# Hybrid decoder step: the sample's page items in the merged attention plan, in one run per round

## The chip, the cores and the metric

One core of a Trainium2 chip runs one launch of the kernel. Its engines are PE (TensorE: matmul and transpose), DVE (VectorE), ACT (ScalarE), POOL (GpSimd) and SP (SyncE, which here issues DMAs). Each engine works through its own list of instructions in order and waits on semaphores for the others. The metric is the time of one execution in microseconds (us); the time before is 1838.18 us, the median of three runs (1833.62 to 1845.4).

## What is computed

One layer of a hybrid decoder over a prompt of 1024 tokens and a sample group of 8 sequences with 8 new tokens each, which read 2048 cached tokens in 16 pages of 128. All inputs are fp32.

```
h_n = rmsnorm(h);  z = h_n @ w_in                    # q,k,v,gates,indexer and HGRN columns
# A: indexer scores pick the top 256 causal keys, then softmax attention over them
s = einsum('bthd,btkhd->bthk', q, k_sel) * HEAD_DIM ** -0.5
p = softmax(where(valid, s, -inf));  att = einsum('bthk,btkhd->bthd', p, v_sel)
# prompt: keys are its own 1024 tokens; sample: 2048 paged cache tokens and its 8 new ones
# B: HGRN2 gated recurrence over chunks, per head a 128 x 128 state
y = sigmoid(ma) * ((att * silu(ga)) @ w_a) + sigmoid(mb) * ((rmsnorm(o) * silu(hg)) @ w_b)
h = h + rmsnorm(y @ w_o);  h = h + sigmoid(h @ w_pg) * (p_i @ w_pp)
```

The kernel does not gather keys: it adds a bias of 0 or -1e30 to the scores and computes attention over all keys up to the diagonal.

## The kernel before

The program runs in stages: norm and transposes of the input, the indexer with its top-k on DVE while PE computes the gate projections, the projections of q, k and v, then **attention**, then HGRN2, merge, and output. The change touches attention only.

**The plan.** Attention is written out as one list `plan` of entries (kind, number, part). PE, ACT and DVE each walk through this one list and do their own part of each entry, so the list sets the order on all three engines.

The prompt's part goes over 32 pairs `att_pairs` (a tile i of 128 queries, and a pair of heads k). They come in groups of eight, tiles 7 and 0 in turn, then 6 and 1, 5 and 2, 4 and 3, so a wide and a narrow pair alternate; tile i has i + 1 blocks of 128 keys. A pair m has two heads, 2m and 2m + 1, called steps. For it:

- Q(m): PE computes the scores of both heads (L1017) and adds the bias (L1022) in four PSUM banks. It waits for both exponentials of pair m - 1, which read the same banks.
- E(2m), E(2m+1): DVE takes the row maximum (L1661, L1662), ACT the exponential with its sum (L1426) into one of three SBUF buffers.
- N(2m), N(2m+1): DVE takes the reciprocal (L1666) and scales the row (L1668).
- T(n, 0), T(n, 1): PE transposes up to four blocks of step n (L1042); ACT copies part 0 out of PSUM (L1432), DVE part 1 (L551), which only tiles 4 to 7 have.
- A(m): when the transposed blocks of both steps are copied, PE multiplies with the values (L1051), and ACT copies the result.

The sample's part is a list `smp_plan` for eight sequences b: K(b, page), PE transposes a page of keys (L1059), copied by ACT (even pages, L1432) or DVE (odd pages, L539); S(b, c), scores against four pages (L1071, L1073), copied by DVE (L542), which also takes a maximum (L1682); X(b), the exponential of the whole row on ACT (L1430, 2112 columns), after a small DVE maximum (L1670, L1671); P(b, c), PE transposes four blocks (L1082), copied by ACT; V(b, c), PE multiplies with four pages of values (L1095); M(b), DVE scales and masks the result (L1676), which PE waits for in O(b) (L1100).

**The ring.** K, S, P, O, T and A write to a ring of three PSUM banks in the order of the plan: PE may start an entry only when the entry three before it has been copied out by its keeper.

**Pages.** SP loads the pages of K, eight ahead, as PE finishes with them (L562); POOL loads the pages of V in the same way. Neither list of loads depends on how prompt and sample are mixed.

**Mixing.** `some(share)` appends sample entries to the plan until they have come as far as the sum of shares given; a round gives 8 shares, and there are 256 entries (without M and X, which come along free) for 32 rounds, so a round takes eight. Round m holds Q(m) and E, N of its steps, the T of the steps of pair m - 1, and A(m - 1).

Of the kernel before, what the change touches and what calls it, by code (L numbers as in the profile page):

```python
# [61 lines left out]
def hybrid_layer(nc, x_p, x_s, p_p, p_s, ck, cv, cki, st, pt, g_pre, g_post, w_in, lbl, hg_g, w_a, w_b, w_o,  # L62
                 w_pg, w_pp, y_p, y_s, k_p, v_p, ki_p, s_p, k_s, v_s, ki_s, s_s):
    with ExitStack() as ctx:
# [313 lines left out]
        NA, NM = len(att_steps), len(att_pairs)  # L378
# [61 lines left out]
        def turns(n):  # L440

            return [("T", n, q) for q in range(att_steps[n][0] // 4 + 1)]

        plan = []
# [3 lines left out]
        def some(share):  # L448

            given[0] += share  # L450
            while given[1] < len(smp_plan) and (sum(e[0] not in "MX" for e in smp_plan[:given[1] + 1])
                                                <= given[0] * n_smp / (8 * NM) or smp_plan[given[1]][0] in "MX"):
                plan.append(smp_plan[given[1]])
                given[1] += 1
        for m in range(NM + 1):
            if m < NM:
                plan += [("Q", m, 0), ("E", 2 * m, 0)]
            some(1)
            plan += turns(2 * m - 2) if m else []
            if m < NM:  # L460
                plan += [("E", 2 * m + 1, 0)]
            some(2)
            if m < NM:
                plan += [("N", 2 * m, 0)]
            plan += turns(2 * m - 1) if m else []
            some(2)
            if m < NM:
                plan += [("N", 2 * m + 1, 0)]
            plan += [("A", m - 1, 0)] if m else []
            some(3)  # L470
        assert given[1] == len(smp_plan)


# [1358 lines left out]
```

How the kernel before makes its waits and increments, by code:

```python
            def run(ins, s_):  # L518
                count[s_.name] = count.get(s_.name, 0) + 1
                ins.then_inc(s_, 1)
                eng.wait_ge(s_, count[s_.name])
# [10 lines left out]
        def ring_copy(eng, run, copy, e):  # L532
            kind, a, x = e
            o, done = ring_bank(e), ring_kept(e)[0]
            eng.wait_ge(sem("ring2_full"), ring_no[e] + 1)
            if kind == "K":
                c = x // 4
                run(copy(KTb[c % 2][:, :, P * (x % 4):P * (x % 4) + P], o.rearrange("p (k t) -> p k t", k=HP)), done)
# [24 lines left out]
        def idx_load(eng, b):  # L564
            for g in range(NPG):
                if b >= NPI and g % 4 == 0:
                    eng.wait_ge(sem("ring_full"), RB + smp_no["T", b - NPI, g // 4] + 1)
                r = eng.value_load(pt_sb[0:1, b * NPG + g:b * NPG + g + 1], min_val=0, max_val=cki.shape[1] - 1)
                eng.dma_start(pgi[b % NPI][:, g, :], cki[0][bass.ds(r, 1), :, :].rearrange("a p d -> p (a d)"))\
                   .then_inc(sem(f"idx_pages{b % NPI}"), 16)
# [27 lines left out]
            def units_to(n):  # L600
                nonlocal nu
                for u in range(nu, min(n, len(units))):
                    mat, kc, c, w = units[u]
                    if u >= NW:
                        sp.wait_ge(*raw_free(u - NW))
                    sp.dma_start(wbuf[u % NW][:, 0:kc, 0:w],
                                 mat[0].rearrange("(k p) n -> p k n", p=P)[:, :, c:c + w])\
                      .then_inc(sem(f"unit_load{u % NW}"), 16)
```

## Time and profile before

| what | before |
|---|---|
| median of three runs | 1838.18 us |
| profiled execution, its time / its span | 1830.32 us / 1828.7 us |
| PE busy | 1640.7 us (90%) |
| DVE busy | 1016.0 us (56%) |
| ACT busy | 466.9 us (26%) |
| POOL busy | 401.1 us (22%) |
| mean granted PE clock | 0.959 of full speed |

The profile is one execution. "Busy" counts instructions in work; matmuls are pipelined, so a busy PE is not PE at its peak. PEld, where it appears, is PE loading the stationary operand, which overlaps its matmuls. The granted clock is the share of 2.4 GHz that PE was allowed; it is 1.0 or 0.5 at any moment. In a row of the timeline, the bracket at the end gives the idle time of the engine before the instruction and what ended it.

### The profile page before, as it was taken

What the parts mean: (1) busy time and instruction counts of PE and PEld (TensorE: products, weight loads), DVE (VectorE), ACT (ScalarE), POOL (GpSimd) and SP (SyncE); (2) the same over time, 40 slices, a digit from 0 to 9 for tenths busy, and PEclk for the clock granted to TensorE, in tenths of its full rate; (3) what the DMA queues carried; (4) which work ended last, traced back from release to release, by engine and by line L of the source; (5) the groups of instructions that cost most, each with busy time, mean ns of one, the idle gap of its engine ahead of it and who ended that gap; (6) DMA issues with size and microseconds to landing.
All of it is one profiled execution on the core that took longest, in us unless ns stands there. A gap on an engine that the chain in (4) does not pass through costs nothing.

```text
span 1828.7 us, 27255 instructions
## 1 busy us (share of the span) xinstructions
PE 1640.7 (90%) x10006; PEld 1259.6 (69%) x10026; DVE 1016.0 (56%) x1778; ACT 466.9 (26%) x816; POOL 401.1 (22%) x431
## 2 busy tenths in 40 slices
PE   3978789999999999997888888877997998999997
PEld 2964569999999999996555555557894663444442
DVE  7258469999999998101556666646963321111111
ACT  5147432223111111011344444541025000101010
POOL 5301333543223223241011121112610000000000
PEclk9988889999999999998889999988998999999999
DMA  5100211223322223013555666624035620010010
GB/s 159 39 6 6 51 38 67 89 96 132 108 96 96 95 96 105 24 50 131 176 175 183 220 218 220 222 85 169 1 88 207 240 96 29 26 52 26 26 45 17
DMA packets 105894, 183.04 MB, mean 100 GB/s; under 512 B 21537, under 2 KB 62050, under 8 KB 105762
## 3 DMA queue, kind: packets, MB, share of 16 engines
q1 hardware_dynamic: 93474, 145.64, 23.7%
q0 software_dynamic: 12288, 35.66, 6.2%
q8 instruction: 80, 1.31, 0.3%
q14 instruction: 52, 0.43, 0.1%
HBM read 147.43 MB, written 33.83 MB: 99 GB/s over the span
## 4 chain that ended last, share of the span: by engine, by line
PE 77%; DVE 10%; issue 5%; ACT 5%; DMA 1%; SPq 0%; POOLq 0%; POOL 0%; ACTq 0%; DVEq 0%; another core or an unknown queue 0%
PE PS L891 36%; PE PS L1233 7%; PE PS L1261 7%; PE PS L898 6%; PE PS L1059 3%; PE PS L1114 2%; DVE buf L1574 2%; PE PS L1256 2%; PE PS L1017 2%; PE PS L1051 2%; PE PS L1071 1%; ACT buf L1432 1%; PE PS L1095 1%; DVE buf L1661 1%; PE PS L1042 1%
## 5 line engine op out<-in xcount | busy, mean ns | idle before, releaser
L891 PE MATMUL PS<-hn_hi,w_hi 128*128 128x384 f32 (+3 forms) x1080 | 353.3, 327 | 6.3 <-issue 6.3
L891 PE MATMUL PS<-hn_lo,w_hi 128*128 128x384 f32 (+3 forms) x1080 | 353.4, 327 | 0.0
L891 PE MATMUL PS<-hn_hi,w_lo 128*128 128x384 f32 (+3 forms) x1080 | 353.4, 327 | 0.0
L1604 DVE TENSOR_SCALAR_CACHE_REDUCE buf<-buf,buf 128x384 f32<-128x384 f32 (+3 forms) x224 | 258.9, 1156 | 8.0
L891 PEld LDWEIGHTS PS<-hn_hi,w_hi 128*128 128x128 f32 (+1 forms) x1080 | 202.4, 187 | 7.2 <-issue 6.5
L891 PEld LDWEIGHTS PS<-hn_lo,w_hi 128*128 128x128 f32 (+1 forms) x1080 | 202.5, 187 | 0.7
L891 PEld LDWEIGHTS PS<-hn_hi,w_lo 128*128 128x128 f32 (+1 forms) x1080 | 202.4, 187 | 0.7
L562 POOL DMA_DIRECT2D buf<-in_cache_v_dram x128 | 70.0, 547 | 332.9 <-PE PS L1095 230.2
L1233 PE MATMUL PS<-buf,buf 128*128 128x512 f32 (+1 forms) x288 | 127.0, 600 | 7.0 <-DVE buf L1789 3.8
L1432 ACT ACTIVATE buf<-PS 128x512 f32<-128x512 f32 (+4 forms) x200 | 101.6, 508 | 101.4 <-PE PS L1059 45.5
L779 POOL CAST w_hi<-buf 128x2048 fp32r<-128x2048 f32 (+1 forms) x27 | 54.2, 2009 | 329.3 <-DMA buf<-in_w_in_dram 200.5
L1661 DVE TENSOR_REDUCE buf<-PS 128x1 f32<-128x1024 f32 (+7 forms) x64 | 48.5, 758 | 139.4 <-PE PS L1022 127.8
L1261 PE MATMUL PS<-buf,buf 128*128 128x512 f32 (+1 forms) x288 | 125.1, 592 | 0.0
L780 POOL TENSOR_TENSOR w_lo<-buf,w_hi 128x2048 fp32r<-128x2048 f32 (+1 forms) x27 | 124.4, 4607 | 2.2
L891 PE MATMUL PS<-buf,buf 128*128 128x384 f32 (+1 forms) x384 | 118.8, 473 | 4.8 <-ACT buf L1466 4.8
L1059 PE MATMUL PS<-buf,buf 128*128 128x128 f32 x512 | 83.3, 303 | 29.0 <-ACT buf L1432 19.0
L891 PEld LDWEIGHTS PS<-buf,buf 128*128 128x128 f32 x384 | 73.7, 192 | 50.5 <-ACT buf L1466 5.8
L1233 PEld LDWEIGHTS PS<-buf,buf 128*128 128x128 f32 (+1 forms) x288 | 53.3, 186 | 79.2 <-issue 70.9
L1261 PEld LDWEIGHTS PS<-buf,buf 128*128 128x128 f32 (+1 forms) x288 | 53.0, 184 | 70.6 <-issue 70.6
L1393 ACT ACTIVATE buf<-PS 128x768 f32<-128x768 f32 x28 | 22.8, 814 | 284.9 <-PE PS L891 284.9
L1059 PEld LDWEIGHTS PS<-buf,buf 128*128 128x128 f32 x512 | 61.4, 153 | 47.1 <-issue 36.2
L1803 DVE TENSOR_TENSOR buf<-PS,buf 128x1024 f32<-128x1024 f32 (+1 forms) x9 | 11.0, 1223 | 144.9 <-ACT buf L1497 144.9
(255 smaller groups left out, 2669.5 us busy)
## 6 DMA issues: line engine op xcount, KB each, us to landing
buf<-in_cache_v_dram POOLq DMA_DIRECT2D x128, 256.0 KB, 4.1
buf<-in_cache_k_dram SPq DMA_DIRECT2D x128, 256.0 KB, 4.1
buf<-in_w_in_dram SPq DMA_DIRECT2D x26, 1024.0 KB, 6.1
gates_scratch<-buf SPq DMA_DIRECT2D x40, 544.0 KB, 3.1
buf<-gates_scratch SPq DMA_DIRECT2D x40, 544.0 KB, 6.2
buf<-in_x_prompt_dram SPq DMA_DIRECT2D x16, 512.0 KB, 4.1
out_dram<-buf SPq DMA_DIRECT2D x2, 2048.0 KB, 8.0
buf<-in_w_out_dram SPq DMA_DIRECT2D x1, 4096.0 KB, 16.6
```

What stands on the lines that cost most here:

```text
L562: eng.dma_start(dst, cache[0][bass.ds(r, 1), :, :, :].rearrange("a p h d -> p (a h d)")).then_inc(s_, 16)
L779: run(nc.gpsimd.tensor_copy(hi, raw), s_)
L780: run(nc.gpsimd.tensor_tensor(lo, raw, hi.bitcast(fp32), ALU.subtract), sem("w_split"))
L891: last = mm(ps[0:min(w, P), 512 * j:512 * j + tn], wt[:, k, P * half:min(w, P * half + P)], xt_[:, k, t0:t0 + tn], start=m == 0, stop=m == ...
L898: last = mm(ps[0:r, WC * j:WC * j + w], xt_[:, k, P * i:P * i + r], wt[:, k, 0:w], start=m == 0, stop=m == len(steps) - 1)
L1017: mm(bank(2 * e, 2)[:, c:c + w], qT[p0:p0 + 64, k, P * i:P * i + P], KT[p0:p0 + 64, k, c:c + w], start=True, stop=False)
L1059: last = tr(o[:, k, :], kpage[n % NKP][:, P * k:P * k + P], ident)
L1233: last = mm(bank(c)[0:r, :], mixT[:, k, P * i:P * i + r], wo[:, k, 512 * c:512 * c + 512], start=k == 0, stop=k == KD - 1)
L1261: last = mm(bank(4 + c)[0:r, :], hT[:, k, 0:r], wpg[:, k, 512 * c:512 * c + 512], start=k == 0, stop=k == KD - 1)
L1432: ring_copy(act, run, lambda o, i: A(o, i, ACT.Copy), e)
L1604: run(V.tensor_scalar(junk[0:r, 0:v.shape[1]], v, t, None, op, ALU.add, accum_out=CN[0:r, j:j + 1]), ch)
L1661: run(V.tensor_reduce(mx[:, q:q + 1], bank(2 * (b % 2), 2)[:, 0:nk], AX.X, ALU.max), ch)
```

## The change

In each round the shares 1, 2, 2 and 3, which stood at four places between the prompt's entries, become one run of 8 shares at the end of the round, after A(m - 1). N(2m) follows E(2m + 1) directly. The set of entries is the same, and so is the order within the prompt's and within the sample's entries.

```diff
         for m in range(NM + 1):
             if m < NM:
                 plan += [("Q", m, 0), ("E", 2 * m, 0)]
-            some(1)
             plan += turns(2 * m - 2) if m else []
             if m < NM:
-                plan += [("E", 2 * m + 1, 0)]
-            some(2)
-            if m < NM:
-                plan += [("N", 2 * m, 0)]
+                plan += [("E", 2 * m + 1, 0), ("N", 2 * m, 0)]
             plan += turns(2 * m - 1) if m else []
-            some(2)
             if m < NM:
                 plan += [("N", 2 * m + 1, 0)]
             plan += [("A", m - 1, 0)] if m else []
-            some(3)
+            some(8)
```

The changed file is five lines shorter from there on, so that L1017 of before is L1012 after, and so on. Buffers in the rows below: 49 is the identity, 131 the queries (and attention outputs), 132 the keys, 134 to 136 the three probability buffers, 137 and 138 their transposed copies, 139 and 140 the transposed key pages, 141 and 142 the transposed sample probabilities, 143 the sample's probability row.

PE in round 14 (m = 14, tile 6), from the first matmul behind Q(14) on. Before:

```order
L1095 MATMUL PS<-buf_161,buf_142 32x128 x4
L1095 MATMUL PS<-buf_162,buf_142 32x128 x4
L1095 MATMUL PS<-buf_163,buf_142 32x128 x4
L1095 MATMUL PS<-buf_164,buf_142 32x128 x4
L1042 MATMUL PS<-buf_49,buf_136 128x128 x2
L1082 MATMUL PS<-buf_49,buf_143 64x128
L1071 MATMUL PS<-buf_132,buf_175 32x64 x4
L1073 MATMUL PS<-buf_114,buf_55 128x64
L1042 MATMUL PS<-buf_49,buf_134 128x128 x2
L1095 MATMUL PS<-buf_133,buf_141 32x128 x4
L1059 MATMUL PS<-buf_49,buf_169 128x128 x4
L1051 MATMUL PS<-buf_137,buf_133 64x128
```

After, from the same place on:

```order
L1037 MATMUL PS<-buf_49,buf_136 128x128 x2
L1037 MATMUL PS<-buf_49,buf_134 128x128 x2
L1046 MATMUL PS<-buf_137,buf_133 64x128
L1046 MATMUL PS<-buf_138,buf_133 64x128
L1046 MATMUL PS<-buf_137,buf_133 64x128
L1046 MATMUL PS<-buf_138,buf_133 64x128
L1090 MATMUL PS<-buf_161,buf_142 32x128 x4
L1090 MATMUL PS<-buf_162,buf_142 32x128 x4
L1090 MATMUL PS<-buf_163,buf_142 32x128 x4
L1090 MATMUL PS<-buf_164,buf_142 32x128 x4
L1077 MATMUL PS<-buf_49,buf_143 64x128
L1066 MATMUL PS<-buf_132,buf_175 32x64 x4
```

Before, V, T(26) (buf_136), P, S, T(27) (buf_134), V and K stand between Q and A(13), whose first matmul is the last row (L1051, buf_137); after, the two T stand there alone, A (L1046) follows, and then V, P, the second V (not shown) and four K.

ACT in the same round and into round 15. Before (L1426 is E, L1430 is X):

```order
L1426 ACTIVATE buf_136,buf_147<-PS,buf_146 128x896
L1432 ACTIVATE buf_141<-PS 64x128
L1432 ACTIVATE buf_138<-PS 128x256
L1430 ACTIVATE buf_143,buf_151<-buf_143,buf_150 128x2112
L1432 ACTIVATE buf_139<-PS 128x4x128
L1432 ACTIVATE buf_131<-PS 128x128
L1432 ACTIVATE buf_139<-PS 128x4x128
L1426 ACTIVATE buf_134,buf_147<-PS,buf_146 128x256
L1432 ACTIVATE buf_137<-PS 128x512
L1426 ACTIVATE buf_135,buf_147<-PS,buf_146 128x256
L1432 ACTIVATE buf_141<-PS 128x512
L1432 ACTIVATE buf_138<-PS 128x512
```

After (L1421 is E, L1425 is X):

```order
L1421 ACTIVATE buf_136,buf_147<-PS,buf_146 128x896
L1427 ACTIVATE buf_138<-PS 128x256
L1427 ACTIVATE buf_131<-PS 128x128
L1427 ACTIVATE buf_141<-PS 64x128
L1425 ACTIVATE buf_143,buf_151<-buf_143,buf_150 128x2112
L1427 ACTIVATE buf_139<-PS 128x4x128 x2
L1421 ACTIVATE buf_134,buf_147<-PS,buf_146 128x256
L1427 ACTIVATE buf_137<-PS 128x512
L1421 ACTIVATE buf_135,buf_147<-PS,buf_146 128x256
L1427 ACTIVATE buf_138<-PS 128x512
L1427 ACTIVATE buf_131<-PS 128x128
L1427 ACTIVATE buf_141<-PS 128x512
```

In round 14 the copy of T(27) (to buf_138) came after the sample's P copy (to buf_141) and now comes before it; in round 15 the P copy (to buf_141) that stood between the second exponential and T(29)'s copy to buf_138 now comes after A's copy (to buf_131). The copies of K (to buf_139, buf_140) stand together.

## Rows read from the trace of the kernel before

**Rows 1.** The profile page, part 4, chain that ended last, by engine.

```profile
PE 77%; DVE 10%; issue 5%; ACT 5%; DMA 1%; SPq 0%; POOLq 0%; POOL 0%; ACTq 0%; DVEq 0%; another core or an unknown queue 0%
```

**Rows 2.** Busy times in the attention stretch: stretch, length, engine us (x), PEclk, DMA share, GB/s.

```profile
851.00:1237.00 386.00, 315.97 (x3231) 208.25 (x3253) 218.03 (x472) 173.71 (x346) 69.96 (x128) 0.92 0.59 193
```

**Rows 3.** Waits in that stretch: engine line, awaited; us in total, times, longest.

```profile
PE PS L1059 <- ACT buf L1432: 19.0, 14, 2.1
...
PE PS L1095 <- ACT buf L1432: 14.3, 17, 2.4
...
PE PS L1051 <- DVE buf L551: 3.1, 7, 0.5
```

**Rows 4.** Timeline of round 14: start us, us, engine line op, out<-in, xcount [idle before <-releaser].

```profile
1029.30 1.88 PE L1017 MATMUL PS<-buf,buf 64*128 64x512 f32 x8
...
1031.98 1.08 PE L1095 MATMUL PS<-buf,buf 128*32 128x128 f32 x32
...
1033.14 1.01 ACT L1426 ACTIVATE buf<-PS,buf 128x896 f32<-128x896 f32 x1 [4.61 <-DVE buf L1662]
...
1034.27 0.38 ACT L1432 ACTIVATE buf<-PS 128x256 f32<-128x256 f32 x1
...
1034.69 1.01 ACT L1426 ACTIVATE buf<-PS,buf 128x896 f32<-128x896 f32 x1
...
1035.82 0.69 ACT L1432 ACTIVATE buf<-PS 64x128 f32<-64x128 f32 x2
...
1036.14 0.42 PE L1095 MATMUL PS<-buf,buf 64*32 64x128 f32 x8 [0.93 <-ACT buf L1432]
...
1037.08 0.66 PE L1051 MATMUL PS<-buf,buf 128*64 128x128 f32 x8
...
1039.70 0.91 ACT L1432 ACTIVATE buf<-PS 128x512 f32<-128x512 f32 x2
...
1040.44 1.07 PE L1059 MATMUL PS<-buf,buf 128*128 128x128 f32 x8 [2.12 <-ACT buf L1432]
```

**Rows 5.** Timeline of round 15, PE and ACT.

```profile
1041.44 0.70 PE L1017 MATMUL PS<-buf,buf 64*128 64x256 f32 x4
...
1043.16 0.47 ACT L1426 ACTIVATE buf<-PS,buf 128x256 f32<-128x256 f32 x1 [1.39 <-PE PS L1042]
...
1043.76 0.60 ACT L1432 ACTIVATE buf<-PS 128x512 f32<-128x512 f32 x1
...
1044.50 1.06 PE L1071 MATMUL PS<-buf,buf 128*32 128x512 f32 x8 [0.42 <-ACT buf L1432]
...
1044.80 0.47 ACT L1426 ACTIVATE buf<-PS,buf 128x256 f32<-128x256 f32 x1 [0.45 <-DVE buf L1662]
...
1048.89 1.75 PE L1051 MATMUL PS<-buf,buf 128*64 128x128 f32 x28 [0.50 <-DVE buf L551]
```

**Rows 6.** Timeline of rounds 16 and 17: their Q, an exponential, and Q of round 18.

```profile
1052.03 0.70 PE L1017 MATMUL PS<-buf,buf 64*128 64x512 f32 x2
...
1055.36 0.90 ACT L1426 ACTIVATE buf<-PS,buf 128x768 f32<-128x768 f32 x1 [3.00 <-DVE buf L1662]
...
1061.34 0.59 PE L1017 MATMUL PS<-buf,buf 64*128 64x384 f32 x2
...
1073.49 0.81 PE L1017 MATMUL PS<-buf,buf 64*128 64x512 f32 x2
```

**Rows 7.** Granted clock in two stretches (columns as rows 2); then round 10's timeline.

```profile
858.00:875.00 17.00, 10.38 (x44) 6.54 (x45) 5.29 (x9) 4.06 (x8) 5.36 (x10) 0.50 1.04 387
990.00:1002.00 12.00, 9.91 (x66) 6.32 (x66) 5.25 (x14) 6.20 (x12) 0.78 (x2) 0.72 0.53 154
...
983.06 1.24 PE L1017 MATMUL PS<-buf,buf 64*128 64x512 f32 x4
...
994.49 1.94 PE L1059 MATMUL PS<-buf,buf 128*128 128x128 f32 x8 [1.67 <-ACT buf L1432]
...
996.36 1.23 PE L1017 MATMUL PS<-buf,buf 64*128 64x256 f32 x4
```

## Prediction

> **What bounds the kernel now.** I read the chain of waits first: PE carries 77% of it [rows 1]. The change touches only the attention stretch, which runs from 851 to 1237 us. The busy times of that stretch say more: PE 316.0 of 386.0 us, DVE 218.0, ACT 173.7, granted clock 0.92 [rows 2]. So PE is the engine that the others must keep fed, 70 us of its time there are idle, and since the clock has two levels, 0.92 means that 16% of the stretch (62 us) ran at the half level. The waits say who ends PE's idle time: mostly copies out of PSUM by ACT, ahead of the page transposes (L1059) and the sample's value matmuls (L1095), 33 us of it, while the prompt's value matmuls (L1051, entry A) wait 3 us for DVE's [rows 3]. ACT and DVE each have slack in sum, but within a round they are a chain: scores, maximum (DVE), exponential (ACT), normalisation (DVE), transposes (PE), copies (ACT, DVE), value matmuls (PE). The question is what PE does during that chain.
>
> **What the change removes, adds and moves.** No instruction is added or taken away; K and V pages, ring copies and exponentials keep their number, their sizes and, for the DMA queues, their order, so SP and POOL only follow PE's releases. Busy time stays the same. What moves is eight ring entries per round. Before, one, two and two of them stood between Q(m) and A(m-1) on PE; now nothing does but the transposes of the round before. Rounds repeat with a period of four, so I work out rounds 14 to 17, which took 44.19 us (Q at 1029.30 and 1073.49) [rows 4 to 6]. The order listing shows all three engines' new orders.
>
> Round 14 (even: Q has 7 key tiles, T and A have 2), now 12.14 us. A(13) needs the copies of both transposed blocks. The copy of the second stands on ACT behind both exponentials. Exponential 28 starts 3.84 us after Q (1033.14), its copy comes at 1034.27, exponential 29 at 1034.69, and the next thing ACT does starts at 1035.82 [rows 4]. That next thing was the sample's P copy; it will be T(27)'s, 0.38 us long as the one at 1034.27. A further 0.14 us passes until PE goes (ACT's first K copy of 0.60 us from 1039.70 lets PE start at 1040.44) [rows 4]. So A(13) starts at 1036.34, 7.04 after Q, against 7.78 now (1037.08). The five entries that used to fill the gap are gone: PE is through with Q at 1031.98, with the two short T at about 1032.6 (0.3 us each, an estimate: eight transposes of this size take 1.00 us from 1040.44 to 1041.44), and then waits 3.7 us. After A (0.6) come eight entries: V 1.0 (a row of 1.08, whose end overlaps the next), a short P, S and V of some 1.0 together, then X and four K. X is as late as now: V at 1036.14 to the fourth K, which needs the first K's copy behind X on ACT, is 4.30 us (1040.44) [rows 4], plus 0.5 for that K (eight transposes take 1.00 until Q at 1041.44). Sum 7.04 + 0.6 + 1.0 + 0.65 + 4.30 + 0.5 = 14.1 us, 2.0 more than now.
>
> Round 15 (odd: Q has 2 key tiles, T and A have 7), now 10.59 us. Exponential 30 starts 1.72 after Q, its ACT copy 2.32. The ring has three banks, so the second half of T(29) must wait for that copy, just as S waits at 1044.50 now. Exponential 31 at 1044.80 does not move; T(29)'s copy follows at about 1045.40 (0.60 long, as at 1043.76), and DVE's half ends at about the same time. A(14) starts near 1046.15, 4.7 after Q, against 7.45 (1048.89), after 2.0 us of idle time in two pieces. Then A 1.7, and O, P, S, V, K x4: 0.15 + 0.5 (P is four transposes, as K is) + 1.3 (the row of 1.06 at 1044.50 and a bias matmul) + 1.0 + 2.0 [rows 5]. Sum 11.4, 0.8 more.
>
> Round 16 (5 key tiles), now 9.31 us (1052.03 to 1061.34). Exponential 32 starts at 3.33; it lasts 0.90, and ACT goes on 0.12 after its end, as at 1034.27; a copy of three tiles is between 0.38 and 0.60, say 0.49. So A(15) at 3.33 + 2 x (0.90 + 0.12 + 0.49) + 0.17 = 6.5, A 0.8, then P, S, V, K x4, P: 0.5 + 1.3 + 1.0 + 2.0 + 0.5 = 5.3. Sum 12.6, 3.3 more: here today's round has next to no idle time, and the whole wait for the chain is new. Round 17 (3 key tiles), now 12.15 us: by round 15's chain with tiles one wider, A(16) near 5.0, A 1.5, then S, V, K x4, P, S with 0.4 us before the last S for the copy of its last page: 6.5. Sum 13.0, 0.9 more [rows 6].
>
> That is 7.0 us for four rounds. Rounds 2 to 31 are 7.5 such groups: 53 us. Rounds 0 and 1 are set by the first pages and stay. In rounds 30 and 31 P(7) now follows X(7) with only O between: 3 us more. Together 56 us. Edits at no cost: N earlier on DVE, where only T's copy stands behind it, which I counted; and K pages, which are fetched eight ahead (without that cover each of the four K in a row would wait for its page, as the first ones do at 858 us, but the entries come no faster on average).
>
> **The clock.** At half level the same eight transposes take 1.94 us (994.49) against 1.07 (1040.44) [rows 4, 7]. The mean granted clock from 990 to 1002 us is 0.72, so 6.7 us of the 12 ran at the half level; before it PE had only short waits that lay close together. Round 10, of the same make as round 14, took 13.30 us (983.06 to 996.36) [rows 7], so such a fall costs 1.2 us where the wait for X hides some of it, and up to half its length where PE is the bound; half of 7 us is 3.5. Each even round now gets one idle stretch of about 3.7 us. I take 15 falls at 2.3, the middle of both, 35 us, less what today's falls cost. Of the 62 us at half level some 17 are the wait for the first pages, from 858 to 875 us [rows 7], which stay; the other 45 are six falls of round 10's size, at 1.2 to 1.5 each 8 us. That leaves 27 us. Without a fall beyond today's the term is nothing; with half of all PE work in the stretch at half level it is about 100 (half of 316 us doubled, a third of that behind waits).
>
> The Trainium skill has a rule that speaks against this change: "TensorE: Matmul & The Clock Gate", section "HAM oscillation — how this bites in real kernels", says that a loop of short matmul bursts, each followed by a wait, is throttled again in every iteration. The trace agrees as far as round 10 goes. By that rule each even round falls, which gives 1913; by today's rate of falls it would be 1886.
>
> **Sum.** The profiled execution took 1830.3 us (span 1828.7), 7.9 below the median of the three runs, 1838.2, and 3.3 below their fastest. 1830 + 56 + 27 = 1913; I name 1915, a little toward the median of runs. About 1% is what a measurement can tell from no change.
>
> **The rivals.**
> - Chain exposed, clock as now: 1830 + 56 = 1886. For it: round 14 had waits of 0.9 and 2.1 us [rows 4] and rounds 14 to 17 show no transposes at the half rate. Against: none of these is as long as 3.7. Chance 0.20.
> - Chain exposed, clock low for most of the stretch, because each fall needs a dense run to recover and gets only eight short entries: 1830 + 56 + 100 = 1986. Chance 0.12.
> - Faster: the sample entries stop waiting for copies that stand behind exponentials on ACT. The 33 us of ACT's copies in [rows 3] go, and A hardly waits: 1797. This needs A's wait to stay under 33/31 = 1.1 us a round. ACT's order speaks against it: two exponentials of 1.01 us and two copies lie between the scores and A, and PE has only some 0.6 us of T to put there. Chance 0.04.
> - No change: the waits only change place, so that what A waits the samples save. The samples now wait least where rounds are shortest (round 16), so there is nothing to save there: 1830 to 1845. Chance 0.06.
> - My forecast, 0.58.
>
> **How the numbers follow.** Slower by over 1% in the forecast and the first two rivals: 0.90; within 1% 0.06; faster 0.04. The range leaves out the last two rivals: from 1872 (the groups of four cost 5 us, not 7, and no further falls) to 1985 (nearly the low clock).
>
> **What would show it.** In the changed profile the value matmuls (now L1046) should wait for ACT's copies (L1427), about 3.5 us in even and 1 to 1.5 us in odd rounds, some 80 us in total with the T transposes, where A now waits 3 us for DVE. Waits of V and of K outside X should be nearly gone. The stretch should be 440 to 480 us long, with PE's busy time higher only by the half-clock work, and a granted clock of 0.80 to 0.88. I am wrong on the chain if the stretch grows by less than 30 us, on the clock if its mean stays at 0.92 or goes under 0.75, and altogether if A starts within 5 us of Q in even rounds.

## The result, and the profile after

The changed kernel takes 1918.99 us, the median of four runs (1917.91 to 1925.84), against 1839.87 us for the kernel before in the same comparison: a ratio of 1.044, with a 95% interval of 1.040 to 1.048. It is slower by 79 us, and the prediction named 1915 us. The two profiled executions, from which the rows are, took 1830.32 and 1917.91 us and lie 87.6 us apart: the one of before is among the fastest of its kernel.

| what | before | after |
|---|---|---|
| median of runs | 1839.87 us | 1918.99 us |
| profiled execution, span | 1828.7 us | 1916.3 us |
| mean granted PE clock of the span | 0.959 | 0.933 |

The page of the kernel after, part 4, the chain that ended last, by engine; it answers to [rows 1]:

```profile
PE 76%; DVE 8%; issue 6%; ACT 5%; DMA 1%; SPq 1%; another core or an unknown queue 1%; POOLq 0%; POOL 0%; ACTq 0%; DVEq 0%
```

The chain hides the loss: it still is PE's for three quarters. The stretch tells more. It begins at 851 us in every kernel and is read here up to the end of its last value matmul (A); for the kernel before that is 1239 us, two more than in [rows 2]. The busy times in that stretch, before:

```profile
851.00:1239.00 388.00, 317.67 (x3244) 209.54 (x3264) 218.09 (x473) 173.92 (x347) 69.96 (x128) 0.92 0.59 192
```

And after (stretch, length, then PE, PEld, DVE, ACT and POOL us, clock, DMA share, GB/s):

```profile
851.00:1322.00 471.00, 342.19 (x3246) 225.42 (x3264) 217.76 (x472) 173.81 (x346) 68.71 (x128) 0.87 0.47 158
```

The stretch grew by 83 us. DVE, ACT and POOL did the same work in the same busy time. PE was busy 24.5 us longer, at a clock of 0.87 in place of 0.92, and its idle time went from 70.3 to 128.8 us, 58.5 more. What PE waited for in the stretch, after (engine line, awaited; us in total, times, longest); these answer to [rows 3]:

```profile
PE PS L1046 <- ACT buf L1427: 72.0, 28, 4.1
PE PS L1054 <- ACT buf L1427: 12.9, 6, 2.6
PE PS L1037 <- ACT buf L1427: 11.7, 12, 2.2
...
PE PS L1046 <- DVE buf L546: 5.0, 4, 1.3
...
PE PS L1090 <- ACT buf L1427: 2.1, 4, 0.7
```

A (L1046) now waits 77 us where it waited 4 (3.1 for DVE and, once, 1.0 for ACT), and V (L1090) waits 2 where it waited 14. Round 14 of the kernel after, PE and ACT:

```profile
1059.46 1.88 PE L1012 MATMUL PS<-buf,buf 64*128 64x512 f32 x8
...
1062.04 0.60 PE L1037 MATMUL PS<-buf,buf 128*128 128x128 f32 x4
1063.29 1.01 ACT L1421 ACTIVATE buf<-PS,buf 128x896 f32<-128x896 f32 x1 [4.57 <-DVE buf L1657]
...
1064.42 0.38 ACT L1427 ACTIVATE buf<-PS 128x256 f32<-128x256 f32 x1
1064.84 1.01 ACT L1421 ACTIVATE buf<-PS,buf 128x896 f32<-128x896 f32 x1
...
1065.97 0.38 ACT L1427 ACTIVATE buf<-PS 128x256 f32<-128x256 f32 x1
...
1066.45 0.66 PE L1046 MATMUL PS<-buf,buf 128*64 128x128 f32 x8 [3.81 <-ACT buf L1427]
1067.04 1.37 PE L1090 MATMUL PS<-buf,buf 128*32 128x128 f32 x32
...
1073.87 1.09 PE L1054 MATMUL PS<-buf,buf 128*128 128x128 f32 x4 [1.23 <-ACT buf L1427]
1074.88 1.23 PE L1012 MATMUL PS<-buf,buf 64*128 64x256 f32 x4
```

PE is through with Q(14) and the four short transposes of T at 1062.6 and stands still for 3.81 us, until ACT has done exponential, copy, exponential, copy. The V behind A takes 1.37 us, against 1.08 in [rows 4]: the clock has fallen. Rounds 14 to 21, from Q to Q, after:

```profile
1059.46:1074.88 15.42, 10.22 (x94) 6.95 (x91) 7.53 (x17) 6.85 (x12) 2.68 (x5) 0.77 0.52 173
1074.88:1089.54 14.66, 12.63 (x113) 9.43 (x112) 6.25 (x15) 4.22 (x10) 0.79 (x2) 0.78 0.21 64
1089.54:1104.57 15.03, 11.36 (x90) 6.75 (x90) 6.55 (x12) 4.99 (x11) 2.49 (x6) 0.77 0.47 156
1104.57:1117.35 12.78, 10.27 (x114) 6.48 (x114) 6.89 (x15) 5.20 (x11) 2.63 (x5) 1.00 0.81 288
1117.35:1131.56 14.21, 7.85 (x100) 5.71 (x97) 7.13 (x17) 6.85 (x12) 2.68 (x5) 1.00 0.49 172
...
sum 112.74, PE 85.27 PEld 56.62 DVE 54.18 ACT 42.96 POOL 17.17; mean PE 10.66 PEld 7.08 DVE 6.77 ACT 5.37 POOL 2.15
```

The same eight rounds before, with round 18 alone and the sum:

```profile
1073.49:1085.12 11.63, 8.16 (x100) 5.57 (x97) 7.13 (x17) 6.53 (x12) 2.45 (x4) 1.00 0.59 177
...
sum 88.37, PE 73.60 PEld 48.36 DVE 54.16 ACT 43.01 POOL 17.54; mean PE 9.20 PEld 6.04 DVE 6.77 ACT 5.38 POOL 2.19
```

The eight rounds took 24.4 us more: PE's idle time went from 14.8 to 27.5 us (12.7 more), its busy time from 73.6 to 85.3 (11.7 more). Before, all eight ran at full clock; after, five of them did not. Round 18 is at full clock in both, and shows the exposed chain without the clock: 14.21 us against 11.63, 2.6 more.

### The profile page after: what moved, and what is told of

Its sections match the earlier page's. It is cut to its first block, busy times and chain, and to the rows that moved or that the text cites. A ratio compares the mean times of both kernels' runs of the same rounds, so it can differ in the third digit from the quotient of the medians.

```text
span 1916.3 us, 27255 instructions
## 1 busy us (share of the span) xinstructions
PE 1668.1 (87%) x10006; PEld 1280.0 (67%) x10026; DVE 1015.3 (53%) x1778; ACT 466.4 (24%) x816; POOL 399.5 (21%) x431
## 4 chain that ended last, share of the span: by engine, by line
PE 76%; DVE 8%; issue 6%; ACT 5%; DMA 1%; SPq 1%; another core or an unknown queue 1%; POOLq 0%; POOL 0%; ACTq 0%; DVEq 0%
PE PS L886 34%; PE PS L1228 7%; PE PS L1256 6%; PE PS L893 5%; PE PS L1054 3%; PE PS L1046 2%; PE PS L1066 2%; PE PS L1109 2%; PE PS L1090 2%; PE PS L1251 2%; ACT buf L1427 2%; PE PS L1012 2%; DVE buf L1656 1%; PE PS L1077 1%; DVE buf L1569 1%
## 5 line engine op out<-in xcount | busy, mean ns | idle before, releaser
L557 POOL DMA_DIRECT2D buf<-in_cache_v_dram x128 | 68.7, 537 | 416.1 <-PE PS L1090 312.3
L1427 ACT ACTIVATE buf<-PS 128x512 f32<-128x512 f32 (+4 forms) x200 | 101.5, 507 | 183.9 <-PE PS L1054 88.0
L1046 PE MATMUL PS<-buf,buf 128*64 128x128 f32 x576 | 46.9, 314 | 77.0 <-ACT buf L1427 72.0
L886 PEld LDWEIGHTS PS<-buf,buf 128*128 128x128 f32 x384 | 73.7, 192 | 50.7 <-ACT buf L1461 6.0
L1054 PE MATMUL PS<-buf,buf 128*128 128x128 f32 x512 | 76.4, 299 | 21.9 <-ACT buf L1427 12.9
L1046 PEld LDWEIGHTS PS<-buf,buf 128*64 128x64 f32 x576 | 38.1, 157 | 83.9 <-ACT buf L1427 83.9
```

The costliest lines, as they stand in the source:

```text
L557: eng.dma_start(dst, cache[0][bass.ds(r, 1), :, :, :].rearrange("a p h d -> p (a h d)")).then_inc(s_, 16)
L886: last = mm(ps[0:min(w, P), 512 * j:512 * j + tn], wt[:, k, P * half:min(w, P * half + P)], xt_[:, k, t0:t0 + tn], start=m == 0, stop=m == ...
L1046: last = mm(o[64 * h:64 * h + 64, 0:P], VN[:, j, HD * (2 * k + h):HD * (2 * k + h) + HD], PTp[h][:, j, :], start=j == 0, stop=j == i, skip ...
L1054: last = tr(o[:, k, :], kpage[n % NKP][:, P * k:P * k + P], ident)
L1427: ring_copy(act, run, lambda o, i: A(o, i, ACT.Copy), e)
```

## The experiments

All of them but one change only the order of the plan, and each is a small edit of the changed kernel's round. The loop is written here in one line: Q is Q(m); E0, E1, N0, N1 are E and N of steps 2m and 2m + 1; T0 and T1 are the T of steps 2m - 2 and 2m - 1; A is A(m - 1); a number is so many shares of sample entries. A share is one entry. In this writing the kernel before is `Q E0 1 T0 E1 2 N0 T1 2 N1 A 3`. "Idle" is the stretch's length less PE's busy time in it. Ratios are to the kernel before, each with its 95% interval. The kernel before was measured again beside each group, with medians of 1839.4 us (T ahead, filled, N only, woven), 1841.7 us (first, second and third only, A last) and 1841.5 us (woven again, woven by parity); the ratios go by these.

| kernel | median us | ratio | stretch us | PE idle | PE busy | clock |
|---|---|---|---|---|---|---|
| before | 1839.9 | 1 | 388 | 70.3 | 317.7 | 0.92 |
| after | 1919.0 | 1.044 (1.040 to 1.048) | 471 | 128.8 | 342.2 | 0.87 |
| T ahead | 1848.8 | 1.006 (1.004 to 1.009) | 394 | 84.0 | 310.0 | 0.94 |
| filled | 1892.2 | 1.028 (1.023 to 1.032) | 446 | 78.6 | 309.1 + 58.3 | 0.94 |
| N only | 1836.5 | 0.998 (0.996 to 1.000) | 388 | 66.3 | 321.7 | 0.91 |
| first cover only | 1836.9 | 0.999 (0.997 to 1.001) | 391 | 70.7 | 320.3 | 0.92 |
| second only | 1848.8 | 1.004 (1.002 to 1.006) | 403 | 83.2 | 319.8 | 0.93 |
| third only | 1874.0 | 1.017 (1.013 to 1.022) | 431 | 94.0 | 337.0 | 0.89 |
| A last | 1873.5 | 1.018 (1.014 to 1.022) | 425 | 93.7 | 331.3 | 0.89 |
| woven | 1811.3 | 0.984 (0.980 to 0.988) | 365 | 52.7 | 312.3 | 0.95 |
| woven, again | 1807.4 | 0.983 (0.980 to 0.986) | 361 | 49.4 | 311.7 | 0.97 |
| woven by parity | 1794.9 | 0.975 (0.972 to 0.978) | 351 | 40.9 | 310.1 | 0.97 |

**T ahead: the long run kept, T's copies taken from behind the exponentials.** PE's list is the same as that of the changed kernel, instruction by instruction; only ACT and DVE do their parts in another order (the two changed together, so their shares can't be told apart). If the long run of eight is what costs, this stays slow; if it is A's wait for a copy that stands behind two exponentials, the loss goes.

```diff
-Q E0 T0 E1 N0 T1 N1 A 8
+Q T0 T1 E0 E1 N0 A N1 8
```

> The changed plan, with PE's list untouched (Q, T, T, A, then eight sample entries in one run), but T stands ahead of E, so that ACT and DVE copy the transposed blocks before they turn to the maximum and the exponential. Theory (PE stands in front of A because the copies of T lie behind two exponentials on ACT): A's wait in even rounds falls from 3.8 us to about 1 us (two copies of 0.4 and the time to get there), in odd rounds from 1.0 to 2.0 to about 1. That is some 45 us in the even and up to 15 in the odd rounds, and the clock falls with it, some 20 us. Given back: sample copies now wait behind the exponentials, up to 1 us a round. Together 1840 to 1865 us. Rival 1 (the long run itself costs: four K and their copies in a row, releases of pages in bunches): the run is the same on PE, so at least 1900. Rival 2 (N earlier costs): also unchanged, at least 1900.

It came to 1848.8 us: 70 of the 79 us are gone with not one PE instruction moved. The stretch, and what A (here L1045) still waits for:

```profile
851.00:1245.00 394.00, 309.98 (x3244) 206.80 (x3264) 217.92 (x473) 173.21 (x346) 69.40 (x128) 0.94 0.57 189
```

```profile
PE PS L1045 <- DVE buf L545: 13.8, 16, 1.1
PE PS L1045 <- ACT buf L1426: 13.3, 16, 1.0
```

Its round 14, PE and ACT:

```profile
1034.12 1.88 PE L1011 MATMUL PS<-buf,buf 64*128 64x512 f32 x8
...
1036.70 0.60 PE L1036 MATMUL PS<-buf,buf 128*128 128x128 f32 x4
1037.18 0.80 ACT L1426 ACTIVATE buf<-PS 128x256 f32<-128x256 f32 x2 [3.79 <-PE PS L1036]
1038.01 1.01 ACT L1420 ACTIVATE buf<-PS,buf 128x896 f32<-128x896 f32 x1
1038.08 0.66 PE L1045 MATMUL PS<-buf,buf 128*64 128x128 f32 x8 [0.78 <-ACT buf L1426]
```

Both copies now run before the exponentials, and A starts 3.96 us after Q with 0.78 us of wait, against 6.99 and 3.81. So most of the idle time comes from the order in which ACT and DVE work through their lists. In the kernel after 28 of A's 32 waits end with ACT. With the long run kept as it is, 0.6% is all that is left against the kernel before. Of the 77 us by which the stretch is shorter than after, 45 are idle time and 32 busy time of PE, since the clock came back too (0.94); how much is due to each, the next kernel shows. Its idle time stays 14 us above that of the kernel before; A's short waits, 27 us in 32 rounds where they were 4, more than account for it.

**Filled: the wait kept, PE kept busy in it.** Before A waits, PE does matmuls that nobody reads: 512 columns in bf16, twelve for tiles 0 to 3 and four for the others, into the bank that A then overwrites. This only adds work.

```diff
                 elif kind == "A":
+                    o, (i, k) = ring2(e), att_pairs[b]
+                    for _ in range(12 if i < 4 else 4):
+                        mm(o, identb, mb_p[:, 0:512], start=True, stop=True, skip_group_check=True)
                     for t_ in (turns(2 * b), turns(2 * b + 1)):
                         for t__ in t_:
                             pe.wait_ge(*ring_kept(t__))
-                    o, (i, k) = ring2(e), att_pairs[b]
```

> The changed kernel, and ahead of A, where PE waits, PE also does 12 (even rounds) or 4 (odd rounds) unneeded bf16 matmuls of 512 columns into the PSUM bank that A is about to overwrite, 2.6 and 0.9 us at full clock, less than A's wait of 3.2 to 4.1 and 1.0 to 2.0 us. The waits for copies stay as they are. Theory (56 us of the 81 are PE's idle time in the chain, some 26 us are granted clock lost after it): the clock of the stretch goes from 0.86 to 0.95 or more, A starts as late as before, and the time is 1890 to 1900. Rival (the clock falls but costs nothing, since ACT and DVE set the pace; all is chain): 1915 to 1925. Second rival (idle stretches are not what lowers the clock): the clock stays at 0.86 and the time at 1919.

It has more work to do and is faster than the changed kernel, 1892.2 against 1919.0 us. The stretch, then the added matmuls alone, then A's wait (here L1048):

```profile
851.00:1297.00 446.00, 367.37 (x3487) 234.26 (x3520) 217.88 (x472) 173.89 (x346) 68.92 (x128) 0.94 0.51 167
...
851.00:1297.00 446.00, 58.27 (x243) 25.92 (x256) 0.94 0.51 167
...
PE PS L1048 <- ACT buf L1429: 21.0, 26, 1.6
```

Its round 14:

```profile
1049.54 1.88 PE L1012 MATMUL PS<-buf,buf 64*128 64x512 f32 x8
...
1052.56 2.75 PE L1042 MATMUL PS<-buf,buf 128*128 128x512 bf16 x12
...
1056.58 0.66 PE L1048 MATMUL PS<-buf,buf 128*64 128x128 f32 x8 [1.27 <-ACT buf L1429]
1057.17 1.08 PE L1092 MATMUL PS<-buf,buf 128*32 128x128 f32 x32
```

A starts 7.04 us after Q, as in the kernel after: the chain is as exposed as there. But V behind it takes 1.08 us again, not 1.37, and PE's own work in the stretch (367.4 less 58.3) takes 309.1 us, not 342.2. That separates the two terms. Kept busy, PE saves 33 us on its own work, while its idle time and the added work together are 8 us longer than the idle time after (78.6 and 58.3 against 128.8). Of the 79 us some 25 (27 by the medians, 25 by the stretch) go in all, and the rest is the chain. The clock was expected at 0.95 or more and came to 0.94; its round 15 still has a mean of 0.79.

**N only.** The one edit of the change that has nothing to do with the sample: N(2m) directly behind E(2m + 1).

```diff
-Q E0 T0 E1 N0 T1 N1 A 8
+Q E0 1 T0 E1 N0 2 T1 2 N1 A 3
```

> The kernel before, with N(2m) directly behind E(2m+1) as in the change, and nothing else moved. I costed this edit at nothing: 1835 to 1843. Rival (it is a cause, since DVE stands at the exponential while sample copies queue behind N): 10 us or more slower, up to 0.3 us a round.

1836.5 us, within what can be measured of no change. The edit costs nothing.

**First, second, third cover only.** Each takes one of the three runs that stood between Q and A and puts it behind A, and leaves the other two.

```diff
-Q E0 T0 E1 N0 T1 N1 A 8
+Q E0 T0 E1 2 N0 T1 2 N1 A 4
```

> The kernel before, with only the first share (one entry, between Q and T(2m-2)) moved behind A. In round 14 of the kernel before, A(13) started at 1037.08, while by ACT's chain it could have gone at 1036.3: about 0.7 us of the cover was surplus. Theory (cover is worth what the chain needs and no more): an entry of 0.5 to 1.0 us costs 0 to 0.3 us a round, and a copy less stands before T's on ACT: 1835 to 1848. Rival (each entry between Q and A covers its own length; the loss of 81 us is spread evenly over the five): 1853 to 1860.

```diff
-Q E0 T0 E1 N0 T1 N1 A 8
+Q E0 1 T0 E1 N0 T1 2 N1 A 5
```

> The kernel before, with only the second share (two entries, between T(2m-2) and T(2m-1)) moved behind A, N(2m) with it. Theory: two entries of 1 to 2 us, less the surplus of 0.7 and less their copies, which leave ACT's queue ahead of T(2m-1)'s: some 0.3 to 0.6 us a round, 1845 to 1858. Even-spread rival: 1868 to 1876.

```diff
-Q E0 T0 E1 N0 T1 N1 A 8
+Q E0 1 T0 E1 2 N0 T1 N1 A 5
```

> The kernel before, with only the third share (two entries, between T(2m-1) and A) moved behind A. These two stand behind the last transposes and are the only cover of the copy that A waits for last (0.4 to 0.6 us long, about 1 us from PE's end to PE's start). Theory: it costs the most of the three, 0.7 to 1.1 us a round, 1858 to 1875, and the sum of the three single moves is less than the 81 us of all of them together, since each alone still leaves cover. Even-spread rival: 1868 to 1876, the same as the second share alone.

They cost nothing, 8 us and 32 us. The idea that each entry taken out of the gap costs the same had asked for 1853 to 1860 of the first and 1868 to 1876 of the second, and falls by both; the 1874.0 us of the third lie in its range and in that of the theory, and decide nothing between them. The waits of "third only" (A is L1047):

```profile
PE PS L1047 <- ACT buf L1428: 30.6, 24, 2.5
PE PS L1047 <- DVE buf L547: 15.8, 8, 2.1
```

and of "second only" (S is L1067):

```profile
PE PS L1067 <- ACT buf L1428: 24.2, 20, 2.5
PE PS L1047 <- ACT buf L1428: 16.8, 15, 1.5
```

The third run stood directly ahead of A, behind both T, and without it A waits 46 us. Without the second, the third still covers much of A's wait (16.8 us are left), but S, which comes early in it, has to wait itself (24.2 us): in round 15 for 1.29 us, until ACT has made the copy behind the second exponential. The three together add up to some 40 us where the whole change costs 79. A run that is left can stand in for one that is taken out, until none is left: that would explain the difference, but it was not tried (two runs moved at once, for instance).

**A last: the run of eight ahead of A.** Here PE has all eight entries for the chain, but behind T in the ring.

```diff
-Q E0 T0 E1 N0 T1 N1 A 8
+Q E0 T0 E1 N0 T1 N1 8 A
```

> The changed plan with A(m-1) at the end of the round: the eight sample entries still are one run, but it stands between T and A, inside the gap. Theory: A does not wait any more (under 0.2 us a round). But the run's own copies are queued on ACT and DVE behind both exponentials, and with three banks PE can start only two or three entries before it needs one of T's or theirs, so part of the wait comes back in front of K, P or S, 1 to 1.5 us a round more than in the kernel before: 1855 to 1885. Rival (what matters is only that PE has something to do in the gap): 1830 to 1845.

```profile
PE PS L1065 <- ACT buf L1426: 17.3, 14, 2.2
PE PS L1089 <- ACT buf L1426: 15.6, 16, 1.4
PE PS L1053 <- ACT buf L1426: 15.0, 8, 2.8
```

1873.5 us, and A hardly waits any more (3.9 us). Now the sample's entries do: S (L1065), V (L1089) and K (L1053). The ring has three banks, so an entry soon behind the two T waits for their copies, which on ACT stand behind the exponentials. In its round 16 S waited 1.69 us, for the copy behind the first exponential, and V 0.59 us, for the copy behind the second. Cover behind the T takes off 45 of the 79 us and no more.

**Woven: what the two findings ask for.** T goes ahead of Q, with sample entries between, so that its copies are on ACT and DVE before the exponentials, and two entries lie behind Q.

```diff
-Q E0 T0 E1 N0 T1 N1 A 8
+T0 4 T1 Q E0 2 A E1 N0 2 N1
```

> The opposite of the change: in a round T(2m-2), four sample entries, T(2m-1), Q, E, two sample entries, A, E, N, two sample entries, N. The copies of T then have Q's 2 us as their cover, and the exponentials have A and the samples as theirs. If the chain theory holds, A hardly waits at all and the samples wait little: of the 66 us of idle PE time in the stretch of the kernel before some 20 to 35 go, 1805 to 1820. If the kernel before is bound by the ring or by pages, no gain: 1830 to 1845.

> The woven kernel again, on the same chip as the one beside it: 1808 to 1814.

1811.3 and 1807.4 us: faster than the kernel before by 1.6 and 1.7%. Idle time falls to 53 and 49 us, by 18 and 21, where 20 to 35 were expected of the first; the second run came out 0.6 us under its range.

**Woven by parity.** Even rounds (wide Q, short T) and odd rounds (short Q, wide T) get their own places, and round 0 its own start, since it has no T or A to do while the first pages come.

```diff
-Q E0 T0 E1 N0 T1 N1 A 8
+m == 0: Q 1 E0 3 E1 N0 4 N1
+even:   T0 3 T1 1 Q E0 2 A E1 N0 2 N1
+odd:    T0 1 T1 3 Q 1 E0 E1 1 N0 N1 A 2
```

> The woven order with a place of its own for the entries of the first round, of even and of odd rounds: the first round starts with Q, which needs no page (the woven plan waited for its first page before any score), even rounds are T(2m-2), three entries, T(2m-1), one, Q, E, two, A, E, N, two, N, and odd rounds T(2m-2), one, T(2m-1), three, Q, one, E, E, one, N, N, A, two. Theory: a few us from the start and up to 0.2 us a round: 1800 to 1810. If what is left of idle time is X and the pages, no difference from the woven kernel: 1811.

1794.9 us, 2.5% faster than the kernel before, and 5 us below the lowest that was expected of it.

```profile
851.00:1202.00 351.00, 310.07 (x3275) 199.33 (x3273) 218.41 (x473) 174.12 (x347) 69.17 (x128) 0.97 0.65 212
...
PE PS L1080 <- ACT buf L1453: 11.5, 7, 3.2
PE PS L1080 <- DMA buf<-in_cache_k_dram: 9.0, 3, 7.8
```

What is left of long waits is K (L1080) behind X, and K for its first pages.

## Why the prediction was right, point by point

The measured time lies 4 us over the 1915 us that were named. The mechanism, a new wait of A in every round and a lower clock after it, is the one that the runs show. That the sum came so close is in part luck, as the terms below show.

**PE as the bound, and the chain within a round.** Held. DVE, ACT and POOL kept their busy times, and yet the stretch grew by a fifth.

**Round 14.** A(13) was to start 7.04 us after Q with 3.7 us of wait; it was 6.99 and 3.81. The round was worked out at 14.1 us and took 15.42, at a mean clock of 0.77. Round 18 is of the same make (its Q has one key tile less, its T one more); it ran at full clock throughout and grew by 2.6 us, where the working gave round 14 2.0. The waits of K for the copy behind X were taken to stay: in round 18 they grew from 1.9 to 2.6 us, and in round 14 they fell from 2.12 [rows 4] to 1.23 us. PE works at the half level there and comes to the fourth K later, which fits.

**Round 15.** A(14) was to start 4.7 us after Q; it started after 6.18. The fall of round 14 reached 3 us into this round, so that its T took 2.59 us, and behind A's wait of 2.03 us came a short fall of its own. That an odd round would have one was not in the working. Rounds 13 and 17, odd rounds at full clock, have A at 4.58 and 4.96 us, as worked out (4.7 and near 5.0).

**Round 16.** A(15) was to start after 6.5 us with the whole wait new; it started after 6.27, having waited 3.52.

**The idle term.** 7.0 us for four rounds, 56 in all. Rounds 14 to 17 had 5.8 us more (7.6 before, 13.4 after), rounds 14 to 21 12.7 more, 6.4 for four, and the whole stretch 58.5 more. So rounds 14 to 17 themselves had less new idle time than the 7.0 us worked out, and other rounds made up for it. Of the 3 us put down for P(7) behind X(7), the waits show 2.2 (P, L1077, for X, L1425). "T ahead" shows the cause by experiment: without the exponentials between T and its copy, 45 of the 58.5 us of idle time go.

**The clock term.** 27 us, from 15 falls at 2.3 less today's 8. PE's busy time grew by 24.5 us. Against the 309 us that PE's own work takes where it stays fast ("filled"), the kernel before loses 8.7 and the kernel after 33.1, for 8 and 35 worked out. The size held; the pattern was not one fall to each even round. In rounds 14 to 18 the clock of the kernel after goes like this (stretch, length, then PE, PEld, DVE, ACT and POOL us, clock, DMA share, GB/s):

```profile
1068.00:1077.00 9.00, 7.77 (x51) 5.17 (x44) 3.08 (x10) 3.61 (x5) 2.15 (x4) 0.50 0.62 207
1078.00:1081.00 3.00, 1.03 (x8) 0.61 (x6) 2.55 (x8) 1.59 (x4) 0.00 (x0) 1.00 0.02 8
1082.00:1084.00 2.00, 2.00 (x20) 1.67 (x17) 0.00 (x0) 0.00 (x0) 0.00 (x0) 0.50 0.00 0
1085.00:1095.00 10.00, 7.13 (x75) 4.24 (x73) 5.77 (x10) 3.86 (x7) 2.15 (x4) 1.00 0.52 162
1095.00:1101.00 6.00, 5.19 (x37) 2.41 (x41) 1.30 (x3) 1.55 (x5) 0.00 (x0) 0.50 0.22 82
1102.00:1132.00 30.00, 21.14 (x235) 14.63 (x232) 14.97 (x34) 13.25 (x25) 6.44 (x12) 1.00 0.62 218
```

There are three falls, of some 9 to 10, 3 and 6 us, at the A of rounds 14, 15 and 16 (the last began while A still waited), and none in round 18, where A waited 3.51 us:

```profile
1123.94 0.88 PE L1046 MATMUL PS<-buf,buf 128*64 128x128 f32 x12 [3.51 <-ACT buf L1427]
```

Round by round, 21 of the 32 have a mean clock below 1, against 11 before; rounds 22 and 26 too stay at 1.00. In rounds 14 to 17 PE's busy time grew by 7.9 us, where two falls at 2.3 had been worked out. So the term is an average that came out right, partly by luck: some even rounds had no fall, and odd rounds that were to have none lost time. By the Trainium skill, "TensorE: Matmul & The Clock Gate", section "HAM oscillation — how this bites in real kernels", a loop of bursts and waits is throttled anew in each iteration; here 12 of the 15 even rounds from 2 to 30 had a mean clock below 1, and rounds 18, 22 and 26 did not. "Filled" shows the direction from the other side: with PE kept active in the waits, the mean clock is 0.94.

**The sum.** 1830 + 56 + 27 = 1913, against 1830 + 58.5 + 24.5 = 1913 from the stretch. The profiled execution was 5 us longer than that: its span outside the stretch grew by 4.6 us (from 1440.7 to 1445.3), which the prediction did not have. In the twelve profiles, whose programs are the same outside the stretch, that part takes 1440.7 to 1448.6 us, and the profile before has the least of all; so the runs give no reason to lay this to the change. By the medians the change cost 79 us, between the two profiles 87.6, and 83 had been worked out.

**The rivals.** "Clock as now" (1886) falls by 24.5 us more busy time. "Low clock for most of the stretch" (1986) falls too: a mean of 0.87 leaves 122 of 471 us at half level. "Faster" had one half right, since V's waits did go from 14 to 2 us; but A's wait, 77 us, is 2.4 us a round, over the 1.1 from which it decided. K's waits behind ACT went only from 19.0 to 12.9: six waits of up to 2.6 us are left, and in the rounds read they are the wait behind X. "No change" falls.

**What would show it.** Nearly all of it came: A waited 3.2 to 4.1 us in even rounds, for ACT (L1427), and 1.0 to 2.0 in odd ones, where 1 to 1.5 stood; 89 us in all with T, where "some 80" stood; stretch 471 (440 to 480); clock 0.87 (0.80 to 0.88).

## What to carry to other kernels

Before work that covers a wait is moved, follow the chain that the waiting instruction hangs on through every in-order queue: here a 0.4 us copy stood behind two exponentials of 1 us, and cover ahead of the matmul that needs it was worth 58 us of idle time and 25 us of clock, though ACT and DVE were busy for only 37% and 46% of the stretch after. It is cheaper still to take the copy from behind the exponentials: with the copies ahead of the exponentials in the lists of ACT and DVE, all eight entries in one run cost 9 us (1849), and with the transposes ahead of the scores too, and entries placed where the waits are left, the kernel is faster than before (1795). Price a new idle time on PE twice, once as idle and once for the clock after it, and take the second from the kernel's own rows at either level.

## What the runs showed of the hardware that was not expected

- Matmuls that nobody reads made the kernel faster: 58 us of added PE work, in waits that were there anyway, took 25 us off the stretch (471 to 446), with a mean granted clock of 0.94 instead of 0.87.
- Half clock cost less than half. In the kernel after some 122 us of the stretch ran at the half level (26% of 471, worked out from the mean of 0.87), some 60 more than before, for 24.5 us of busy time: 0.4 us for each. Part of it PE stood still (it was busy for 7.77 of the 9 us from 1068 to 1077), and eight page transposes took 1.94 us at the half level against 1.07 [rows 4, 7], not twice as long.
- The order of work on ACT and DVE alone, with the same list on PE, moved the time by 70 us, 3.8% of the kernel before's.
